# Expert stage: transposes and gathers moved behind the second part of up_a, from PSUM bank 7 to bank 0

## The reference, cut to what matters

```python
def moe_swiglu(hn, router, w1, w3, w2):
    t = hn.reshape(-1, d)
    logits = (t @ router).astype(jnp.float32)
    top_vals, top_idx = lax.top_k(logits, TOP_K)          # 2 of 8 experts for each token
    top_w = jax.nn.softmax(top_vals, axis=-1)
    gates = jnp.sum(top_w[..., None] * jax.nn.one_hot(top_idx, N_EXPERTS), axis=1)
    for e in range(N_EXPERTS):
        h_e = jax.nn.silu(t @ w1[e]) * (t @ w3[e])        # 1024 -> 3584
        out = out + gates[:, e:e + 1] * (h_e @ w2[e])     # 3584 -> 1024
    return out.reshape(bsz, s, d)
```

## Time and profile before

| | |
|---|---|
| three runs | 2828.22, 2829.37, 2835.06 us; median 2829.37 |
| the profiled execution | 2828.22 us, span in the profile 2826.3 us |
| PE busy | 2730.0 us (97%) |
| DVE busy | 1681.8 us (60%) |
| ACT busy | 461.6 us (16%) |
| granted clock | 0.989 of full speed on average |
| HBM | 613.64 MB read |

### The profile page before, as it was taken

One profiled execution on the slowest core, in us unless ns is written; L12 is line 12 of the kernel. 1 busy time (PEld: TensorE's weight loads), 2 busy tenths in 40 slices (PEclk: granted clock), 3 DMA queues, 4 the chain that ended last, 5 costly groups with the idle time before them and its releaser, 6 DMA issues.

```text
span 2826.3 us, 48779 instructions
## 1 busy us (share of the span) xinstructions
PE 2730.0 (97%) x21008; PEld 2100.2 (74%) x21008; DVE 1681.8 (60%) x2917; ACT 461.6 (16%) x914; POOL 90.8 (3%) x130
## 2 busy tenths in 40 slices
PE   7999999999999999999999999989999999999997
PEld 6689877776678979777766887557777777777775
DVE  2554155776265406477554764247778877877875
ACT  2230212101212111200142111211111111111111
POOL 0011300000001120000000000000000000000000
PEclk9999999999999999999999999989999999999999
DMA  6231342543333234444333443328999999999995
GB/s 239 97 149 75 135 162 91 216 165 149 114 136 120 73 125 165 164 165 179 116 146 120 168 152 136 126 106 371 414 376 389 417 379 382 415 380 376 414 418 224
DMA packets 56941, 617.88 MB, mean 219 GB/s; under 512 B 6545, under 2 KB 6801, under 8 KB 8721
## 3 DMA queue, kind: packets, MB, share of 16 engines
q1 hardware_dynamic: 54576, 603.27, 54.2%
q0 software_dynamic: 2144, 11.45, 1.0%
HBM read 613.64 MB, written 1.05 MB: 217 GB/s over the span
## 4 chain that ended last, share of the span: by engine, by line
PE 86%; DVE 7%; DMA 4%; ACT 1%; issue 1%; DVEq 0%; SPq 0%; ACTq 0%
PE ps L1548 11%; PE ps L747 10%; PE ps L1229 10%; PE ps L1098 8%; PE ps L1241 8%; PE ps L1558 7%; PE ps L1572 5%; PE ps L1078 4%; PE ps L770 3%; PE ps L1594 3%; PE ps L728 2%; PE ps L1110 2%; PE ps L813 1%; DMA fbT<-in_od_exp_w 1%; PE ps L1207 1%; PE ps L1249 1%
## 5 line engine op out<-in xcount | busy, mean ns | idle before, releaser
L1098 PE MATMUL ps<-hT,slabA 128*128 128x256 f32 x1024 | 232.0, 381 | 1.1 <-ACT work L1824 1.1
L1098 PEld LDWEIGHTS ps<-hT,slabA 128*128 128x128 f32 x1024 | 192.7, 191 | 27.9 <-ACT work L1824 1.9
L1558 PE MATMUL ps<-fbT,work 128*64 128x256 f32 x1792 | 206.1, 383 | 0.2 <-DMA fbT<-in_od_exp_w 0.2
L1558 PEld LDWEIGHTS ps<-fbT,work 128*64 128x64 f32 x1792 | 124.2, 137 | 68.0 <-issue 11.0
L1548 PE MATMUL ps<-prm,hT 128*64 128x128 f32 x2688 | 168.5, 274 | 5.6 <-DVE resets L2948 5.6
L747 PE MATMUL ps<-hT,slabA 128*128 128x256 f32 x736 | 165.4, 385 | 0.7 <-DMA slabA<-in_od_w_in 0.5
L1548 PEld LDWEIGHTS ps<-prm,hT 128*64 128x64 f32 x2688 | 152.3, 137 | 13.9 <-DVE resets L2948 6.0
L747 PEld LDWEIGHTS ps<-hT,slabA 128*128 128x128 f32 x736 | 140.7, 193 | 20.9 <-issue 1.4
L1229 PEld LDWEIGHTS ps<-work 128*128 128x128 f32 x1152 | 139.5, 192 | 21.5 <-issue 21.0
L1229 PE MATMUL ps<-work 128*128 128x128 f32 x1152 | 144.0, 276 | 0.1
L747 PE MATMUL ps<-slabA,hT 128*128 128x512 f32 (+2 forms) x416 | 141.5, 497 | 2.7 <-ACT work L2011 1.8
(11 more groups left out here) (449 smaller groups left out, 4581.4 us busy)
## 6 DMA issues: line engine op xcount, KB each, us to landing
slabA<-in_od_exp_w SPq DMA_DIRECT2D x56, 2048.0 KB, 11.9
fbT<-in_od_exp_w SPq DMA_DIRECT2D x56, 2048.0 KB, 9.8
slabB<-in_od_exp_w SPq DMA_DIRECT2D x56, 1024.0 KB, 11.4
fbT<-in_od_exp_w SPq DMA_DIRECT2D x56, 1024.0 KB, 12.1
slabA<-in_w_in SPq DMA_DIRECT2D x24, 2048.0 KB, 8.0
slabA<-in_mlp_w SPq DMA_DIRECT2D x16, 2048.0 KB, 9.5
slabB<-in_mlp_w SPq DMA_DIRECT2D x32, 1024.0 KB, 4.8
slabA<-in_ev_ffn_w SPq DMA_DIRECT2D x11, 2048.0 KB, 8.0
```

The costliest lines, as they stand in the source:

```text
L1098: last = mm(ps[:, b, 0:T], side["gates"][:, k, c % 4 * P:(c % 4 + 1) * P], hT[:, k, :], start=(k == 0), stop=(k == KD - 1))
L1558: last = mm(ps[SMALL * j:SMALL * (j + 1), 1, 0:2 * P].rearrange("p (w n) -> p w n", w=2), xs[:, k, :], v[:, k, :, j * P:(j + 1) * P], star ...
```

## The change

`extra` is called behind `up_a` part 1 instead of ahead of it. Its results go to bank 0 instead of bank 7, in all five kinds of step. It waits for `products_out` (the second one of the step) instead of `hidden_b`; `down_b` now waits for `hidden_b` in every step. `up_a` part 0 of the step that follows an extra step waits for `slots_a` instead of `products_out`, and `turn` no longer waits for `slots_a`. On VectorE the reading of what `extra` wrote moves from ahead of `join_up` to behind `rows_a`.

```diff
--- before.py
+++ after.py
@@ -1539,7 +1539,8 @@
                 factors = ((xs[:, 0, :, first], w[:, 0, 0]), (xs[:, 1, :, first], w[:, 0, 1]), (ts_[:, 0], up_a_sums(0)), (ts_[:, 1], up_a_sums(1)),
                            (ts_[:, 2], up_a_sums(2)), (xs[:, 1, :, second], up_a_sums(3)), (ts_[:, 3], w[:, 1, 1]))
                 if g or part:
-                    pe.wait_ge(sem("products_out"), due("pe", "products_out"))
+                    free = "slots_a" if part == 0 and (g - 1) % UPS in extras(g - 1) else "products_out"
+                    pe.wait_ge(sem(free), due("pe", free))
                 for c, (lhs, rhs) in enumerate(factors[4 * part:4 * part + 4]):
                     if c == 2 and part == 0:
                         pe.wait_ge(sem("sums_ready"), due("pe", "sums_ready"))
@@ -1575,8 +1576,6 @@
 
             def turn(g):
 
-                if g % UPS in extras(g):
-                    pe.wait_ge(sem("slots_a"), due("pe", "slots_a"))
                 pe.wait_ge(sem("hidden_a"), due("pe", "hidden_a"))
                 for half in range(2):
                     tr(ps[:, 7, half * P:(half + 1) * P], rows_a(g)[:, half, :], P)
@@ -1586,8 +1585,7 @@
             def down_b(g):
 
                 w2 = down_rings[1].take(pe).rearrange("p (j n) -> p j n", j=2)
-                if (g + 1) % UPS not in extras(g + 1):
-                    pe.wait_ge(sem("hidden_b"), due("pe", "hidden_b"))
+                pe.wait_ge(sem("hidden_b"), due("pe", "hidden_b"))
                 he = hidden_b(g).rearrange("p (j c) -> p j c", j=2)
                 for j in range(2):
                     for half in range(2):
@@ -1616,14 +1614,14 @@
                 pe.wait_ge(sem("pick_gates"), due("pe", "pick_gates", len(parts) * NT))
                 for i, s in enumerate(parts):
                     for t in range(NT):
-                        last = tr(ps[:, 7, (2 * i + t) * P:(2 * i + t + 1) * P], pick_gate[:, s, t, :], P)
+                        last = tr(ps[:, 0, (2 * i + t) * P:(2 * i + t + 1) * P], pick_gate[:, s, t, :], P)
                 last.then_inc(sem("slots_a_psum"), up("slots_a_psum"))
 
             def extra(g):
 
                 p, i = divmod(g, UPS)
                 if i in extras(g):
-                    pe.wait_ge(sem("hidden_b"), due("pe", "hidden_b"))
+                    pe.wait_ge(sem("products_out"), due("pe", "products_out"))
                 if i == 5:
                     turn_spread((0, 1))
                 if i == 6:
@@ -1632,9 +1630,9 @@
                     if i == 8:
                         pe.wait_ge(sem("picked"), due("pe", "picked", 2 * NT))
                     if i in (8, 9):
-                        gather_a(p + 1, range(4 * (i - 8), 4 * (i - 8) + 4), 15 - i)
+                        gather_a(p + 1, range(4 * (i - 8), 4 * (i - 8) + 4), 8 - i)
                     if i == 10:
-                        gather_b(p + 1, 7)
+                        gather_b(p + 1, 0)
 
             def scatter(bank, order, done):
 
@@ -1672,8 +1670,8 @@
                     if g == 0:
                         pe.wait_ge(sem("slots_a"), due("pe", "slots_a"))
                     up_b(g)
+                    up_a(g, 1)
                     extra(g)
-                    up_a(g, 1)
                     if g:
                         down_a(g - 1)
                         down_b(g - 1)
@@ -2921,7 +2919,7 @@
 
                 def take_spread(s0, n):
                     dve.wait_ge(sem("slots_a_psum"), due("dve", "slots_a_psum"))
-                    v.tensor_copy(spread[:, s0:s0 + n, :].rearrange("p s t -> p (s t)"), ps[:, 7, 0:n * T]).then_inc(sem("slots_a"), up("slots_a"))
+                    v.tensor_copy(spread[:, s0:s0 + n, :].rearrange("p s t -> p (s t)"), ps[:, 0, 0:n * T]).then_inc(sem("slots_a"), up("slots_a"))
                     dve.wait_ge(sem("slots_a"), at("slots_a"))
 
                 def sums_of_slots(p):
@@ -3026,14 +3024,6 @@
                         gate_a(p, i - 3)
                     if i == 5:
                         gate_b(p)
-                        take_spread(0, 2)
-                    if i == 6:
-                        take_spread(2, 1)
-                    if p < PAIRS - 1:
-                        if i in (8, 9):
-                            take_slots_a(p + 1, range(4 * (i - 8), 4 * (i - 8) + 4), 7)
-                        if i == 10:
-                            take_slots_b(p + 1, 7)
                     dve.wait_ge(sem("products_out"), due("dve", "products_out"))
                     join_up()
                     if g + 1 < PAIRS * UPS:
@@ -3041,8 +3031,17 @@
                     dve.wait_ge(sem("silu_a"), due("dve", "silu_a"))
                     v.tensor_tensor(rows_a(g), silu_a(g), joined_a[:, 2:4, :], ALU.mult).then_inc(sem("hidden_a"), up("hidden_a"))
                     dve.wait_ge(sem("hidden_a"), at("hidden_a"))
-                    if p < PAIRS - 1 and i == 9:
-                        sums_of_slots(p + 1)
+                    if i == 5:
+                        take_spread(0, 2)
+                    if i == 6:
+                        take_spread(2, 1)
+                    if p < PAIRS - 1:
+                        if i in (8, 9):
+                            take_slots_a(p + 1, range(4 * (i - 8), 4 * (i - 8) + 4), 0)
+                        if i == 9:
+                            sums_of_slots(p + 1)
+                        if i == 10:
+                            take_slots_b(p + 1, 0)
                 dve.wait_ge(sem("down_a"), due("dve", "down_a"))
                 down_sums_of(PAIRS * UPS - 1)
                 turned(PAIRS * UPS - 1)
```

## The result

The changed kernel takes 2852.57 us (median of six runs, 2846.33 to 2859.75); the kernel before takes 2832.38 us in the runs made beside it (six with the three shown above, 2828.22 to 2838.22). The ratio is 1.0072, with a 95% interval of 1.0055 to 1.0087: slower, by 15.6 to 24.6 us. Six more executions of the changed kernel took 2849.01 to 2856.93 us; all twelve together have the same median. The forecast was 2845 us with a range to 2851, so the direction and the mechanism came out, and the time lies 1.6 us above the range.

A forecast was written before the change was run, and what follows sets the result against it. TensorE was taken to bound the kernel, busy 97% of the span. Waits of 13.8 us for ScalarE's copy and 2.4 us for VectorE sum to 16.2 us on 2828.22: 2844.4, taken as 2845 us, range 2838 to 2851.

The forecast's parts named there:

- What bounds the stage: Expert stage: TensorE sets the pace, busy 901.11 of 926 us, waiting for transfers only 1.4 and 0.2 us.
- The old position costs 0.10 us and no wait: Extra work ahead of `up_a` part 1: moving to it costs 0.10 us, so the change relieves no stall.
- First wait: Extra work behind `up_a` part 1 waits for ScalarE's copy of bank 0: 0.81 us in 17 steps, 13.8 us.
- Second wait: `up_a` part 0 after i=5 waits for VectorE's reading of bank 0: 0.28, 1.15, 0.69, 0.33 us, together 2.4 us.
- i=6 just makes it: After i=6, VectorE's half-size copy ends at about +12.1 and TensorE wants bank 0 at +12.20: no wait counted.
- Transfers give nothing back: Earlier release of the `up_a` slab could return at most 1.6 us of transfer waits; nothing credited.
- Sum: Whole change: 13.8 + 2.4 = 16.2 us on the profiled execution's 2828.22 us, giving 2844.4.
- From the sum to the time: Whole kernel: three-run median is 1.15 us above the profiled run, so 2845 us; highest sum 2848, range to 2851.
- Transfers hiding the stall: Expert stage paced by DMA: TensorE's pauses only replace waits for weights, time stays at about 2829 us; chance 0.05.
- VectorE late everywhere: Every extra step as late as the worst i=5 (1.15 us): cost 33.3 us, time 2863 us; chance 0.04.
- Clock: TensorE's added pauses lower its granted clock: seventeen drops, 28 us more, time 2873 us; chance 0.02.
- First wait unseen: ScalarE's copy is out before TensorE's extra work arrives, leaving only the wait for VectorE: 2832 us; chance 0.02.

## Why the prediction was wrong, point by point

- **What bounds the stage.** Right. Plain steps kept 14.94 us, TensorE's waits reached the end in full, and no transfer hid them.
- **The old position costs 0.10 us and no wait.** Right: moved late in bank 7, the kernel is as fast as before.
- **First wait, 17 x 0.81 = 13.8 us.** Right mechanism, 0.09 too large each: 17 x 0.72 = 12.2 us. The row that served as model is 0.1 us later, since the late semaphore comes second there; with it first TensorE's start is 0.82 and not 0.92 us late, and 0.82 - 0.10 is 0.72.
- **Second wait, 2.4 us in i=5.** Right place and four times, mis-sized: 0.45, 0.90, 1.17, 0.72 us, 3.2 in all. I took 0.1 us for the semaphore where this order of waits has 0.15, and credited TensorE's start with 0.81 instead of 0.72 us; how late VectorE is, since it waits for the next slab, also differs between executions by more than that.
- **i=6 just makes it.** Wrong: 0.2 us in each of the four, 0.8 in all, the bound I had named. By the prediction's own figures the copy ended at +12.1 and the semaphore took 0.1 us more, against +12.20 for TensorE: nothing was left between them, and the term was put at nothing.
- **Transfers give nothing back.** Within its bound: the sum of what plain steps exceed 14.94 us fell by 0.7 us, and varies from profile to profile (2.4 and 3.9 us in two of before).
- **Sum.** 12.2 + 3.2 + 0.8 - 0.7 = 15.5 us in the stage, for 16.2. That it comes so near is luck: the first wait was 1.6 us too large, the second and i=6 together 1.6 too small.
- **From the sum to the time: the step that failed.** I set the sum on the median of three runs, 2829.37, and allowed about 3 us above the highest sum ("a few us") for a median, although one of the three runs lay 5.7 us above their own. That base was 4 us low: 23 runs of the same kernel give 2833.43, other 23 give 2834.09. 2833.4 + 15.5 is 2849, inside the range. The range treated the spread of whole executions as a small addition to the mechanism's bounds, and it is as wide as they are.
- **What is left over.** All 18 runs of the changed kernel have a median of 2851.95, 3 us above that 2849. They also have a lower mean clock, 0.9866 against 0.9872 in 57 runs of the kernel before. At the same mean clock of 0.987 the two kernels are 15.4 us apart (2849.88 in 4 runs, 2834.49 in 24), and 15.3 to 17.3 at the other values, about what the stage lost. From 1935 to 2780 us the clock reads 1.00 in both kernels. That points at the clock outside those steps; where, and whether it is chance or belongs to the change, no run shows.
- **Rivals.** Transfers hiding the stall: excluded by the step lengths. VectorE late everywhere: no, i=8 to 10 show one wait only. Clock: not behind pauses of 0.65 us; the stage reads 1.00. First wait unseen: no, 17 rows.

## What to carry to other kernels

A PSUM bank that is filled and copied in turn is free for other work only between the copy and the next filling; before giving it a second user, lay the copy and the new reader on the timeline of the engine that is full, and put work of that engine that doesn't need the bank beside each of them. When TensorE is 97% busy, 0.7 us of waiting in 17 of 56 steps is readable in the step lengths to 0.01 us, while whole runs need many repetitions to show it: predict a stage from its steps, and take the base, and its spread, from more than three runs.

## What had not been expected of the hardware

- Two waits in sequence, ahead of `up_a` part 0: with the late semaphore second, TensorE starts 0.15 us behind the releaser, with it first 0.05 us.
- Executions of one unchanged program spread over 12 to 15 us (2828.34 to 2843.18 in 23 runs), and the slowest have the lowest mean clock (0.988 to 0.984). Part of the spread lies ahead of the stage, in code that no edit touches. One early stretch does not settle it: from 40 to 60 us the clock reads 0.83 in the first profile of before and also in the one of bank 0 in the old place, whose stage begins 8.4 us later, at 1925.00.
- A single pause of 3.47 us cost 5.2 us, since 1.7 us came on top at a clock of 0.79; 49 pauses of 0.65 us listed in one stretch left the clock at 1.00.
